# Earlier bank copies, a later second cache batch, and probabilities scaled on VectorE in a hybrid decoder step

## The chip, the cores and the metric

The kernel runs on one core of a Trainium2 chip. The metric is the device time of one execution in microseconds, as the median of several. The engines are named as the profile names them: PE is TensorE, DVE is VectorE, ACT is ScalarE, POOL is GpSimd, and SP is the SyncE queue that issues most transfers.

## What is computed

Two decoder layers over a prompt of 512 tokens and over 8 single sample tokens, each with a paged cache of 256 past tokens. Half of a layer's heads are sparse attention (an indexer picks the keys, 8 heads of 64), half are retention. Cut to what matters:

```
def trunk_layer(x, l, pos, mixer_a, s0, ...):
    h = rmsnorm(x, g_mix_pre[l])
    qa, ka, va, qi, ki, wi, qb, kb, vb, gb = project_mixers(h, w_in[l], pos)   # rope on q and k
    a = mixer_a(qa, ka, va, qi, ki, wi)          # keys by the indexer, then softmax attention
    b, S = retention_mixer(qb, kb, vb, gb, s0, g_ret[l])
    m = jnp.concatenate([a, b], axis=-1) @ w_out[l]
    x = x + rmsnorm(m, g_mix_post[l])
    f = jnp.square(jax.nn.relu(rmsnorm(x, g_ffn_pre[l]) @ w_up[l])) @ w_down[l]
    return x + rmsnorm(f, g_ffn_post[l]), ...

def sparse_attend(q, kg, vg, valid):
    s = einsum('bthd,btkhd->bthk', q, kg) * HEAD_DIM ** -0.5
    p = softmax(where(valid, s, -inf))
    return einsum('bthk,btkhd->bthd', p, vg)
```

The prompt's top 128 scores of each query are found in rounds of eight (a maximum of eight values, then their replacement) and turned into a mask that is added to the attention scores. All numbers are fp32.

## The kernel before

**Chunks and blocks.** The combined input projection is worked off in 8 chunks of 512 columns: 0 indexer, 1 q_a, 2 k_a, 3 v_a, 4 q_b, 5 k_b, 6 gate, 7 v_b. The chunks 0 to 3, 6 and 7 have five blocks, four tiles of 128 prompt tokens and one of the 8 sample tokens, with eight k-steps each (`project`). The chunks 4 and 5 are computed by a Strassen-like scheme with seven products and the sample block, in the order `BLOCKS = (1, 0, 2, 6, 5, 7, 3, 4)` (`project_blocks`); (4,0) is product 1, (4,1) the sample block, (4,2) product 2, and so on. Blocks alternate between two PSUM banks, so block i can start only when block i-2 has been copied out of its bank (`bank_taken`): (4,1) waits for the copy of (3,4), (4,2) for `take_p1(4)`, (5,0) for `chunk_c12(4)` on VectorE, (5,2) for `take_p1(5)`, (5,3) for `evacuate(5, 1)`.

**What runs beside the blocks.** Each engine's order is written out by hand. On TensorE a function `beside_*` is called after every k-step and puts in other work: transposes, the cache batches and the attention of the prompt. The sample tokens' attention goes over two batches of four samples, once for the scores (keys, `beside_v`, L944 and L952) and once for the values (`beside_qb`, L1025). The cache tiles lie in a ring of four (`cring`), so SP loads each next four only when `cache_used` has counted the batch before; key tiles 0 to 3 and 4 to 7, then value tiles 8 to 11, then the weight units 10 and 11, then value tiles 12 to 15, then the state and unit 12 stand in this order on SP's queue.

**Attention steps.** The 32 tiles of prompt attention (4 query blocks of 8 heads) go through 36 steps, spread over `ATT_BLOCKS`, the blocks (4,6) to (6,4). `head_steps(c, i)` gives a block's steps and the k-step behind which each stands: (4,6) has steps 0 and 1 behind k=3 and k=7, (4,7) steps 2 and 3, (5,0) 4 and 5, (5,1) only 6, (5,2) 7 and 8, and so on; (6,0) to (6,3) have four steps each, (6,1) steps 23 to 26, and (6,4) has step 35. The function `attend(i)` on each engine does its share of step i:

- TensorE: for odd i the products with the values of tiles i-5 and i-4 (L970); for even i the scores of tiles i and i+1 (L983); then the transposes of tile i-3 (L993), which wait for `p_ready` and, in the first two, for `om_ready`, the end of `own_values(1)`.
- VectorE: for even i the masks and row maxima of tiles i and i+1 (L1884); then the reciprocal of the row sum of tile i-1 (L1897).
- ScalarE: the copy of the transposed tile i-3 (L1441), the exponential of tile i (L1446), and the scaling of tile i-1 by the reciprocal (L1454), which raises `p_ready`. The last of these, on ScalarE:

```
if 1 <= i <= NT * NH:
    j = i - 1
    p = p_sb[j % P_SLOTS][:, 0:(j // NH + 1) * P]
    act.wait_ge(r_ready, past(r_ready) + j + 1)
    nc.scalar.activation(p, p, ACT.Copy, scale=rinv[:, j % 2:j % 2 + 1]).then_inc(p_ready, 1)
```

A tile is 128 rows by 128, 256, 384 or 512 columns, for query block 0 to 3. Between the steps `beside` puts in other work: on ScalarE the copies of PSUM banks (`take_p1`, `evacuate`, `take_first`, `take_p5`, `scale_quad`), on VectorE the sums of the Strassen scheme (`chunk_*`), the rotations (`rope(c, t)`, four operations), the parts of the gate's sigmoid (`sigmoid(t, part)`: an addition and half of the reciprocal, the other half, the product with the gate) and `decayed_keys`. On GpSimd run the weight sums of the chunks 4 and 5 (L2439) and the gate's products with its gain (L2473).

Every instruction that another one waits for raises a semaphore, and an engine works off its queue in order.

## Time and profile before

| | us |
|---|---|
| median of three runs | 1595.49 (1593.41 to 1599.24) |
| profiled execution | 1598.03 |
| its span | 1596.3 |
| its mean granted TensorE clock | 0.993 |
| PE busy in the span | 1555.8 |
| VectorE, ScalarE, GpSimd busy | 814.3, 488.0, 475.1 |

The profile is one execution, with every instruction's start and duration. Its time is the span and 1.7 us around it. A wait is idle time of an engine, put down to what ended last before the engine went on. TensorE's durations are modelled at their ends, so successive ones overlap a little, and starts are the better measure. The two layers run the same program, the first from the start to about 790 us and the second from there; the stretch of chunks 3 to 6 begins at about 110 us and at about 900 us.

### The profile page before, as it was taken

The page shows a single profiled execution, that of the slowest core. Times are in us where ns is not written, and L with a number is a line of the kernel's source. Part 1 is how long each engine was busy: PE and PEld are TensorE (multiplying, and loading weights), DVE is VectorE, ACT ScalarE, POOL GpSimd, SP SyncE. Part 2 cuts the span into 40 slices and gives each one's busy share as a digit, 9 for nine tenths or more (in the row PEclk, how much of TensorE's full clock was granted, in tenths as well). Part 3 has the DMA queues.
Part 4 walks back from the last instruction along what each step waited for, and adds up shares of the span by engine and source line. Part 5 has one row for each costly group of instructions (what it writes and reads, how often), then busy time and mean ns, then how long its engine had stood idle before and what let it go on. Part 6 is the DMA issues. An engine that isn't in the chain of part 4 may idle for free.

```text
span 1596.3 us, 21682 instructions
## 1 busy us (share of the span) xinstructions
PE 1555.8 (97%) x7966; PEld 1159.2 (73%) x7966; DVE 814.3 (51%) x1644; ACT 488.0 (31%) x1109; POOL 475.1 (30%) x354
## 2 busy tenths in 40 slices
PE   8999899999999999999999998999999999999998
PEld 5445664688888888888844456546888888888887
DVE  4698466864653003333467964578566520133334
ACT  5222366324421002310242224772254210032101
POOL 0005201123564324444310042010236534233461
PEclk9999999999999999999999989999999999999999
DMA  6316310123331222212223263100234321222211
GB/s 222 123 62 214 131 54 1 55 84 106 132 125 61 106 100 85 80 62 97 93 70 106 80 210 108 54 34 22 84 125 139 106 92 68 106 83 102 79 54 54
DMA packets 52812, 150.41 MB, mean 94 GB/s; under 512 B 8250, under 2 KB 29506, under 8 KB 39394
## 3 DMA queue, kind: packets, MB, share of 16 engines
q1 hardware_dynamic: 45218, 140.65, 25.5%
q10 hardware_dynamic: 7488, 8.36, 1.5%
q8 instruction: 64, 1.05, 0.3%
q14 instruction: 42, 0.34, 0.1%
HBM read 139.79 MB, written 9.02 MB: 93 GB/s over the span
## 4 chain that ended last, share of the span: by engine, by line
PE 79%; DVE 13%; ACT 3%; issue 2%; DMA 1%; SPq 1%; POOL 1%; ACTq 0%; DVEq 0%; POOLq 0%
PE ps L1183 45%; PE ps L807 10%; PE ps L1121 7%; PE ps L844 5%; DVE arena L1870 2%; DVE top L1868 2%; PE ps L785 1%; PE ps L772 1%; PE ps L970 1%; PE ps L993 1%; PE ps L983 1%; DVE x_feat L2020 1%; PE ps L1079 1%; ACT arena L1346 1%; DVE arena L1816 1%
## 5 line engine op out<-in xcount | busy, mean ns | idle before, releaser
L807 PE MATMUL ps<-wring,h_feat 128*128 128x512 f32 (+1 forms) x704 | 316.0, 586 | 3.0 <-ACT h_feat L1306 2.2
L1183 PE MATMUL ps<-arena,wring 128*128 128x256 f32 (+1 forms) x1280 | 285.8, 382 | 0.3 <-DVE arena L2104 0.3
L1183 PEld LDWEIGHTS ps<-arena,wring 128*128 128x128 f32 x1280 | 243.0, 190 | 37.8 <-DVE arena L2104 1.1
L807 PEld LDWEIGHTS ps<-wring,h_feat 128*128 128x128 f32 x704 | 124.7, 190 | 125.5 <-issue 112.5
L2403 POOL TENSOR_TENSOR wring<-wring,arena 128x512 f32<-128x512 f32 (+1 forms) x48 | 78.7, 1639 | 346.8 <-PE ps L1183 323.5
L1183 PE MATMUL ps<-h_feat,wring 128*128 128x256 f32 (+1 forms) x768 | 176.6, 381 | 0.0
L1183 PEld LDWEIGHTS ps<-h_feat,wring 128*128 128x128 f32 x768 | 145.9, 190 | 21.6
L1183 PE MATMUL ps<-mix,wring 128*128 128x256 f32 (+1 forms) x512 | 120.3, 383 | 1.5 <-DVE p_sb L2078 1.5
L1183 PE MATMUL ps<-arena 128*128 128x264 f32 x512 | 119.2, 386 | 0.0
L1121 PE MATMUL ps<-mix,wring 128*128 128x256 f32 (+1 forms) x512 | 115.1, 384 | 0.9 <-ACT mix L1473 0.8
L2386 POOL TENSOR_TENSOR pt_sb<-pt_sb 128x256 f32<-128x256 f32 (+1 forms) x94 | 72.7, 773 | 126.5 <-ACT pt_sb L1280 123.0
L1183 PEld LDWEIGHTS ps<-mix,wring 128*128 128x128 f32 x512 | 97.1, 190 | 17.3 <-DVE p_sb L2078 2.3
L1183 PEld LDWEIGHTS ps<-arena 128*128 128x128 f32 x512 | 97.3, 190 | 16.4
L1121 PEld LDWEIGHTS ps<-mix,wring 128*128 128x128 f32 x512 | 96.5, 190 | 15.8 <-issue 1.2
L1346 ACT ACTIVATE arena<-ps,rtok 8x128 f32<-8x128 f32 (+3 forms) x112 | 54.7, 488 | 157.0 <-PE ps L807 148.7
L1514 ACT ACTIVATE arena<-arena 128x264 f32<-128x264 f32 (+1 forms) x96 | 40.6, 423 | 182.9 <-DVE arena L2104 131.7
L2403 POOL TENSOR_TENSOR arena<-wring 128x512 f32<-128x512 f32 (+1 forms) x48 | 79.2, 1650 | 35.0 <-DMA wring<-in_w_all 24.4
L2403 POOL TENSOR_TENSOR wring<-wring 128x512 f32<-128x512 f32 (+1 forms) x48 | 79.6, 1658 | 3.8
L2403 POOL TENSOR_TENSOR arena<-arena,wring 128x512 f32<-128x512 f32 (+1 forms) x48 | 79.2, 1649 | 3.8
L2457 POOL COPY arena<-kTs 128x4 f32<-128x4 f32 x16 | 3.5, 216 | 228.0 <-ACT kTs L1574 219.2
L1491 ACT ACTIVATE p1s<-ps 128x256 f32<-128x256 f32 x40 | 15.4, 385 | 162.2 <-PE ps L1183 162.1
L1183 PE MATMUL ps<-h_feat,arena 128*128 128x264 f32 x256 | 62.2, 386 | 0.0
(251 smaller groups left out, 2106.1 us busy)
## 6 DMA issues: line engine op xcount, KB each, us to landing
wring<-in_w_all SPq DMA_DIRECT2D x108, 1024.0 KB, 5.1
arena<-in_cache_k SPq DMA_DIRECT2D x32, 256.0 KB, 5.2
arena<-in_cache_v SPq DMA_DIRECT2D x32, 256.0 KB, 4.3
o_k_out<-arena ACTq DMA_DIRECT2D x2, 1024.0 KB
o_v_out<-arena ACTq DMA_DIRECT2D x2, 1024.0 KB
arena<-in_state SPq DMA_DIRECT2D x2, 1024.0 KB, 4.8
o_rets_out<-arena ACTq DMA_DIRECT2D x2, 1024.0 KB, 9.6
wring<-in_w_idx SPq DMA_DIRECT2D x3, 648.0 KB, 5.3
```

The source lines that it names most:

```text
L772: last = mm(ps[:, bank_of(0, t), 0:W_IDX], h_feat[:, k, token_cols(t)], wt, start=(k == 0), stop=(k == KD - 1))
L785: last = mm(ps[32 * g:32 * g + NB, bank_of(c, i), 0:c1 - c0], h_feat[:, k, SEQ:TOK], wt[:, (k % 4) * width + c0:(k % 4) * width + c1], sta ...
L807: last = mm(ps[:, bank_of(c, i), 0:width], h_feat[:, k, token_cols(t)], wt, start=(k == 0), stop=(k == KD - 1))
L844: last = mm(product_bank(c, n)[:, t, :], b, a, start=(opens(n) and k == 0), stop=(j == 3), skip_group_check=True)
L1121: last = mm(ps[:, item_bank(n), 0:span(h)], wring[u % SLOTS][:, (m % 2 * KD + k) * P:(m % 2 * KD + k + 1) * P], mix[:, k, HALVES[h]], star ...
L1183: last = mm(out, a[:, j, :], b, start=(opens(n) and j == 0), stop=(j == nk - 1), skip_group_check=True)
L1346: nc.scalar.activation(dst[:, c0:c1], ps[rr, bank_of(c, i), 0:c1 - c0], ACT.Copy, scale=rtok[rr, sc, t:t + 1]).then_inc(done, 1)
L1514: nc.scalar.activation(f, f, ACT.Relu).then_inc(act_step, 1)
L1868: v.max(t8, w).then_inc(dve_step, 1)
L1870: v.match_replace(w, t8, w, MARK).then_inc(dve_step, 1)
L2386: nc.gpsimd.tensor_tensor(ssum[:, hc], ssum[:, hc], sqr[added % 2][:, 0:span(h)], ALU.add).then_inc(sq_used, 1)
L2403: nc.gpsimd.tensor_tensor(dst, in0, in1, op).then_inc(s_ready, 1)
```

## The change

1. TensorE: the second batch of cache scores (`sample_scores(1)`) goes from behind block (3,4) to behind k=3 of (4,0).
2. TensorE: the second batch of cache values goes from behind (4,5) to behind k=5 of (4,6).
3. ScalarE: the copy of block (3,4) goes ahead of the two exponentials of the sample scores. VectorE does nine selection rounds ahead of the maxima of these scores instead of eight, then two, then four instead of five.
4. ScalarE: `take_p1(5)`, `evacuate(5, 1)`, `take_first(5)` and `take_p5(5)` go ahead of the first attention step of their block (`ahead`). In chunk 6 `scale_quad(5, "21")` goes from (6,1) to behind the second step of (6,0). 
5. VectorE: `own_values(1)` goes from ahead of all attention steps to behind step 2, ahead of `chunk_c12(4)`.
6. VectorE: `rope(5, 0)` goes from behind step 23 to behind step 22 and `rope(5, 1)` from behind step 26 to behind step 23; each part of the sigmoid goes one step on.
7. The scaling of the probabilities goes from ScalarE to VectorE, behind the reciprocal; the semaphore `r_ready` falls away.

The diff, without the unchanged body of `sample_scores`:

```
@@ TensorE
-                if (i, k) in ((2, KD - 1), (4, KD - 1)):
-                    g = (i - 2) // 2
+                if (i, k) == (2, KD - 1):
+                    sample_scores(0)
+
+            def sample_scores(g):
...
             def beside_qb(i, k):
+                if (i, k) == (0, 3):
+                    sample_scores(1)
...
-                if (i, k) in ((3, KD - 1), (5, KD - 1)):
-                    g = (i - 3) // 2
+                if (i, k) in ((3, KD - 1), (6, 5)):
+                    g = (i - 3) // 3
@@ ScalarE
-            def beside(c, i):
-
-                if (c, i) == (4, 7):
-                    scale_quad(4, "22", proj_c22)
-                if (c, i) == (5, 0):
-                    scale_quad(4, "12", proj_c12)
+            def ahead(c, i):
+
                 if (c, i) == (5, 1):
                     take_p1(5)
-                    act.wait_ge(as_mm, past(as_mm) + 1)
-                    nc.scalar.activation(mix[:, 0:4, SEQ:TOK], ps[:, 7, 0:4 * NB].rearrange("p (h b) -> p h b", b=NB), ACT.Copy).then_inc(as_read, 1)
-                    act.wait_ge(as_read, up(as_read))
-                    scale_quad(4, "21", proj_c21)
                 if (c, i) == (5, 2):
                     evacuate(5, 1)
                 if (c, i) == (5, 3):
                     take_first(5)
                 if (c, i) == (5, 5):
                     take_p5(5)
-                if (c, i) == (5, 7):
+
+            def beside(c, i, s):
+
+                if (c, i, s) == (4, 7, 0):
+                    scale_quad(4, "22", proj_c22)
+                if (c, i, s) == (5, 0, 0):
+                    scale_quad(4, "12", proj_c12)
+                if (c, i, s) == (5, 1, 0):
+                    act.wait_ge(as_mm, past(as_mm) + 1)
+                    nc.scalar.activation(mix[:, 0:4, SEQ:TOK], ps[:, 7, 0:4 * NB].rearrange("p (h b) -> p h b", b=NB), ACT.Copy).then_inc(as_read, 1)
+                    act.wait_ge(as_read, up(as_read))
+                    scale_quad(4, "21", proj_c21)
+                if (c, i, s) == (5, 7, 0):
                     scale_quad(5, "22", proj_c22)
-                if (c, i) == (6, 0):
+                if (c, i, s) == (6, 0, 0):
                     scale_quad(5, "12", proj_c12)
-                if (c, i) == (6, 1):
-                    evacuate(6, 0)
+                if (c, i, s) == (6, 0, 1):
                     scale_quad(5, "21", proj_c21)
-                if c == 6 and i > 1:
+                if c == 6 and i and s == 0:
                     evacuate(6, i - 1)
...
-                if 1 <= i <= NT * NH:
-                    j = i - 1
-                    p = p_sb[j % P_SLOTS][:, 0:(j // NH + 1) * P]
-                    act.wait_ge(r_ready, past(r_ready) + j + 1)
-                    nc.scalar.activation(p, p, ACT.Copy, scale=rinv[:, j % 2:j % 2 + 1]).then_inc(p_ready, 1)
-                    act.wait_ge(p_ready, up(p_ready))
...
                 evacuate(3, 3)
+                evacuate(3, 4)
                 for g in range(2):
                     act.wait_ge(smx_ready, past(smx_ready) + g + 1)
...
-                evacuate(3, 4)
...
                 for c, i in ATT_BLOCKS:
                     steps = head_steps(c, i)
+                    ahead(c, i)
                     for s, (slot, step) in enumerate(steps):
                         attend(step)
-                        if s == 0:
-                            beside(c, i)
+                        beside(c, i, s)
@@ VectorE
                 if 1 <= i <= NT * NH:
                     j = i - 1
+                    n, c = (j // NH + 1) * P, j % 2
                     dve.wait_ge(p_exp, past(p_exp) + j + 1)
-                    v.reciprocal(rinv[:, j % 2:j % 2 + 1], rsum[:, j % P_SLOTS:j % P_SLOTS + 1]).then_inc(r_ready, 1)
-                    dve.wait_ge(r_ready, up(r_ready))
+                    v.reciprocal(rinv[:, c:c + 1], rsum[:, j % P_SLOTS:j % P_SLOTS + 1]).then_inc(dve_step, 1)
+                    dve.wait_ge(dve_step, up(dve_step))
+                    p = p_sb[j % P_SLOTS][:, 0:n]
+                    v.tensor_scalar(p, p, rinv[:, c:c + 1], None, ALU.mult).then_inc(p_ready, 1)
+                    dve.wait_ge(p_ready, up(p_ready))
...
                 if (c, i, s) == (4, 7, 0):
+                    own_values(1)
                     chunk_c12(4)
...
                     if s == 0:
                         chunk_c21(5)
                         rope(5, NT)
-                    if s in (1, 2):
-                        rope(5, 1 + s)
-                if c == 6 and i and s < 3:
-                    sigmoid(i - 1, s)
+                    else:
+                        rope(5, (None, 2, 3, 0)[s])
                 if (c, i, s) == (6, 1, 0):
-                    rope(5, 0)
-                if (c, i, s) == (6, 1, 3):
                     rope(5, 1)
+                if c == 6 and i and s:
+                    sigmoid(i - 1, s - 1)
...
-                select_top(sc[3], top8[:], 8)
+                select_top(sc[3], top8[:], 9)
...
-                select_top(sc[3], top8[:], 5)
+                select_top(sc[3], top8[:], 4)
...
-                own_values(1)
...
-                        for part in range(len(steps), 3):
+                        for part in range(len(steps) - 1, 3):
                             sigmoid(i - 1, part)
                         decayed_keys(i - 1)
```

## Rows read from the trace of the kernel before

**Rows 1.** First part of the page: busy us, share of the span, instructions
```profile
PE 1555.8 (97%) x7966; PEld 1159.2 (73%) x7966; DVE 814.3 (51%) x1644; ACT 488.0 (31%) x1109; POOL 475.1 (30%) x354
```

**Rows 2.** Waits of PE: line, released by, us in total, times, longest
```profile
PE ps L1025 <- DMA arena<-in_cache_v: 4.5, 2, 2.6
...
PE ps L785 <- ACT arena L1346: 4.1, 2, 2.3
...
PE ps L844 <- ACT arena L1360: 4.0, 2, 2.0
...
PE ps L970 <- ACT pt_sb L1441: 3.9, 6, 1.2
...
PE ps L983 <- DVE neg_mx L1884: 3.0, 2, 1.5
...
PE ps L952 <- DMA arena<-in_cache_k: 1.9, 2, 1.1
```

**Rows 3.** Windows: stretch, us, busy us of each engine, PEclk, DMA share, GB/s
```profile
168.00:171.00 3.00, 2.96 (x16) 0.68 (x16) 0.00 (x0) 0.00 (x0) 0.00 (x0) 0.50 0.00 0
...
936.00:946.00 10.00, 10.00 (x54) 5.62 (x47) 6.71 (x15) 3.22 (x7) 2.34 (x1) 0.50 0.89 338
...
251.50:266.30 14.80, 13.34 (x70) 6.39 (x69) 11.87 (x24) 11.10 (x21) 1.51 (x1) 1.00 0.00 1
```

**Rows 4.** Timeline of PE, layer one: start, duration, operation, count, [idle before, releaser]
```profile
148.83 2.43 PE L844 MATMUL ps<-wring,h_feat 128*128 128x256 f32 x10
...
152.82 3.62 PE L844 MATMUL ps<-arena,mix 128*128 128x256 f32 x16
...
168.04 3.50 PE L1025 MATMUL ps<-arena 128*32 128x512 f32 x16 [2.64 <-DMA arena<-in_cache_v]
...
177.47 0.49 PE L983 MATMUL ps<-arena 64*128 64x128 f32 x4
...
179.83 1.92 PE L844 MATMUL ps<-wring,h_feat 128*128 128x256 f32 x8
...
191.03 3.12 PE L844 MATMUL ps<-wring,h_feat 128*128 128x256 f32 x8 [2.01 <-ACT arena L1360]
...
198.15 1.99 PE L844 MATMUL ps<-arena,mix 128*128 128x256 f32 x8 [0.29 <-ACT arena L1346]
...
203.52 1.99 PE L844 MATMUL ps<-arena 128*128 128x256 f32 x8
```

**Rows 5.** Timeline of PE, layer two
```profile
947.92 3.62 PE L844 MATMUL ps<-arena,mix 128*128 128x256 f32 x16
...
962.38 1.92 PE L1025 MATMUL ps<-arena 128*32 128x512 f32 x16 [1.89 <-DMA arena<-in_cache_v]
```

**Rows 6.** Timeline of ACT, layer one, then layer two
```profile
143.25 1.54 ACT L1346 ACTIVATE arena<-ps,rtok 8x128 f32<-8x128 f32 x4
...
146.29 0.60 ACT L1360 ACTIVATE arena<-ps 128x512 f32<-128x512 f32 x1 [1.49 <-issue]
...
935.98 0.60 ACT L1360 ACTIVATE arena<-ps 128x512 f32<-128x512 f32 x1 [1.00 <-ACT arena L1346]
```

**Rows 7.** Timeline of DVE, layer one
```profile
127.92 0.69 DVE L1868 MAX8 top<-arena 128x8 f32<-128x512 f32 x1
...
140.06 0.42 DVE L2237 TENSOR_REDUCE mxs<-ps 128x1 f32<-128x257 f32 x1
...
178.95 0.69 DVE L1841 TENSOR_TENSOR arena<-ps,arena 128x512 f32<-128x512 f32 x1
...
190.21 0.93 DVE L1810 TENSOR_TENSOR rstd_ffn<-arena,sinT 128x256 f32<-128x256 f32 x1
```

**Rows 8.** Groups: count | busy us, mean ns | idle before, releaser
```profile
L1454 ACT ACTIVATE p_more<-p_more,rinv 128x512 f32<-128x512 f32 x8 | 5.8, 724 | 6.4 <-DVE rinv L1897 6.2
...
L1856 DVE TENSOR_SCALAR arena<-s_sb,wi 128x512 f32<-128x512 f32 x2 | 1.0, 486 | 0.7 <-ACT s_sb L1548 0.7
```

**Rows 9.** Timeline of POOL, layer one
```profile
188.52 2.34 POOL L2439 TENSOR_TENSOR wring<-wring 128x1024 f32<-128x1024 f32 x1 [21.62 <-PE ps L785]
```

More of the change, by code:

```diff
@@ L240 @@
     stat_mm=6, st_mm=168, tok_std=6, proj_read=32, proj_p1=2, proj_c11=2, proj_p5=2, proj_u2=2, proj_u3=2, proj_c22=2, proj_c12=2,
-    proj_c21=2, proj_scaled=6, in_sums=4, chunk_sums=8, r_ready=32, tr_read=19, ts_read=3, dot_read=12, srelu_done=1,
+    proj_c21=2, proj_scaled=6, in_sums=4, chunk_sums=8, tr_read=19, ts_read=3, dot_read=12, srelu_done=1,
     wm_ready=1, sp_exp=2, vrep_ready=2, spt_ready=1, p_exp=32, pt_ready=32, as_read=1, blk_read=4, gate_exp=5,
@@ L446, in build @@
         chunk_sums = sem("chunk_sums")
-        r_ready = sem("r_ready")
         rope_done = sem("rope_done")
@@ L938, in beside_v @@
                     transpose_group(zr[0], *pairs[2 + k // 2])
-                if (i, k) in ((2, KD - 1), (4, KD - 1)):
-                    g = (i - 2) // 2
-                    if g == 0:
-                        pe.wait_ge(sbias_ready, past(sbias_ready) + 1)
-                    mm(ps[:, 2 + g, 0:L], exps[:, g, :], bias_s[:], start=True, stop=False, skip_group_check=True)
-                    for b in range(4 * g, 4 * g + 4):
-                        pe.wait_ge(c_slot[b % CSLOTS], past(c_slot[b % CSLOTS]) + 16 * NPAGES * (b // CSLOTS + 1))
-                        pe.wait_ge(knew_done, past(knew_done) + b + 1)
-                    for h in range(4):
-                        for b in range(4 * g, 4 * g + 4):
-                            q4 = 32 * (b % 4)
-                            kc = cring[b % CSLOTS][:].rearrange("p (h k) -> p h k", k=L)
-                            last = mm(ps[q4:q4 + 32, 2 + g, 0:L], qs[:, b, 32 * h:32 * h + 32], kc[:, h, :],
-                                      start=False, stop=(h == 3), skip_group_check=True)
-                            if h == 3:
-                                last.then_inc(cache_used, 1)
+                if (i, k) == (2, KD - 1):
+                    sample_scores(0)
+            def sample_scores(g):
+                if g == 0:
+                    pe.wait_ge(sbias_ready, past(sbias_ready) + 1)
+                mm(ps[:, 2 + g, 0:L], exps[:, g, :], bias_s[:], start=True, stop=False, skip_group_check=True)
+                for b in range(4 * g, 4 * g + 4):
+                    pe.wait_ge(c_slot[b % CSLOTS], past(c_slot[b % CSLOTS]) + 16 * NPAGES * (b // CSLOTS + 1))
+                    pe.wait_ge(knew_done, past(knew_done) + b + 1)
+                for h in range(4):
+                    for b in range(4 * g, 4 * g + 4):
+                        q4 = 32 * (b % 4)
+                        kc = cring[b % CSLOTS][:].rearrange("p (h k) -> p h k", k=L)
+                        last = mm(ps[q4:q4 + 32, 2 + g, 0:L], qs[:, b, 32 * h:32 * h + 32], kc[:, h, :],
+                                  start=False, stop=(h == 3), skip_group_check=True)
+                        if h == 3:
+                            last.then_inc(cache_used, 1)
             def attend(i):
```

## The prediction

> **What bounds the kernel now.** I read the busy times first: TensorE (PE) is busy 97% of the span, VectorE 51%, ScalarE 31% [rows 1]. So time can only come out of TensorE's idle stretches and out of stretches where its clock is low. The waits of PE come next [rows 2]. In the part that the change touches (chunks 3 to 6 of the projection, about 135 to 285 us in the first layer and 925 to 1078 us in the second) six of them sum to 4.5 + 4.1 + 4.0 + 3.9 + 3.0 + 1.9 = 21.4 us over both layers; total less longest gives the other layer's share. Then the windows: behind the wait at 166 us the granted clock was 0.50 (the 1.2 GHz level) for 3 us, and in the second layer it was 0.50 over all of 936 to 946 us [rows 3]. The timeline gives the price of that: 16 products of L1025 took 3.50 us behind the 2.64 us wait at 168.04, and 1.92 us at full clock in the second layer [rows 4, 5]. The waits before the low stretches were 2.0 (twice), 2.3 and 2.6 us; the 1.8 us wait of the first layer at 144.9 and the 1.9 us one at 962.4 had none behind them. A wait of 2 us or more thus costs more than itself here.
>
> **The change part by part.** (c,i) is block i of chunk c. Terms are per layer.
>
> *A, opening of chunk 4.* The second batch of cache scores moves behind four of eight k-steps of (4,0), about 1.9 us later, which hides its wait for the key cache (1.1 and 0.8 us) [rows 2]. The copy of (3,4) moves ahead of the two exponentials; before, TensorE waited for it at (4,1) (1.8 and 2.3 us) [rows 2]. That would bring (4,2) forward to 148.83 - 1.1 - 1.8 = 145.9 [rows 4]. What is late next is take_p1(4), which frees the bank of (4,2). ScalarE reached it at 146.29 [rows 6]. The exponentials now come one selection round later, (140.06 - 127.92)/8 = 1.52 us [rows 7]; the four pieces of the copy, 1.54 us, leave the queue between them and take_p1 [rows 6]. The two cancel: take_p1(4) still starts at 146.3, ends at 146.85, and (4,2) starts at 146.9, with a new wait of 1.0 us. Gain 1.9 us in layer one. In layer two take_p1(4) started at 935.98 [rows 6], so (4,2) can start at 936.6 and (4,3) after the undisturbed length 152.82 - 148.83 = 4.0 us, at 940.6 instead of 947.92 [rows 4, 5]: gain 7.3 us, most of it the low clock. The value cache's transfers wait for the batch and leave 0.7 us later; the first group that needs them stands some 14 us behind, which covers that. The weight units 10 and 11 queued behind them on SP's queue are needed later still.
>
> *B, second value batch,* from behind (4,5) to k=5 of (4,6). Four k-steps (1.99 us), the step-0 products (0.49) and two k-steps more (1.0) stand in between, 3.4 us, against a wait of 2.6 and 1.9 us [rows 2, 4]. Its transfers are started by the first value batch, which moves with TensorE, so the wait goes and some 0.8 us is to spare. Gain: 2.64 + (3.50 - 1.92) = 4.2 us in layer one, 1.9 us in layer two [rows 4, 5].
>
> *C, own_values(1)* moves from ahead of the attention steps to behind step 2 on VectorE, ahead of chunk_c12(4). Behind it wait the first transposes on TensorE (step 3) and, behind those, (5,0), whose bank chunk_c12(4) frees. Before, step 2 started at 177.47, chunk_c12(4) on VectorE at 178.95, (5,0) at 179.83 [rows 4, 7]. Now 0.33 us of scaling (two more rows down) and 1.44 us of own_values (two operations of 0.69 with gaps) stand ahead of chunk_c12(4) and its 0.69: it ends 1.48 + 0.33 + 1.44 + 0.69 = 3.95 us after step 2, and (5,0) starts at 4.0 instead of 2.36. Loss 1.7 us, as 1.0 us ahead of the transposes and 0.6 behind them.
>
> *D, banks copied ahead.* take_p1(5), evacuate(5,1), take_first(5) and take_p5(5) no longer stand behind the copy and exponential of their first step. Before, take_p1(5) started only after step 6, and (5,2) waited 2.0 us in both layers [rows 2, 4]. Now its product is done one block (about 4 us) before (5,2), and it ends some 2 us early. The price is that the attention copies stand behind them: evacuate(5,1), 1.54 us [rows 6], delays the copy of step 7. TensorE needs that copy two steps later (5 us), so it is covered. Behind the wait (5,2) ran low: 8 products in 3.12 us against 1.99, and block (5,2) lasted 198.15 - 191.03 = 7.12 us against 203.52 - 198.15 = 5.37 for (5,3), which does the same [rows 4]. Gain 2.01 + 1.75 = 3.8 us, and the second layer repeats it.
>
> *E, chunk 6: scaling on VectorE, rotations ahead of the sigmoid.* ScalarE loses 32 scalings per layer, 0.73 us at 512 columns [rows 8]. The nearest row for them on VectorE is the multiply by a column at L1856, 0.49 us for 512 [rows 8]; I put 0.29, 0.35, 0.42 and 0.49 for the four widths, 12.4 us per layer, where VectorE idles about half the time. Upper bound: 0.69, what a two-input operation of that size takes [rows 7]. The waits here were 3.0 us for VectorE's maxima and 3.9 us for ScalarE's copies, over both layers [rows 2]. The first stood behind a sigmoid part and a rotation between steps 23 and 24; now only a rotation (about 2.2 us) stands there and step 24's maxima precede the sigmoid. The second arose because ScalarE's scaling waited for VectorE's reciprocal (6.2 us of such waits at L1454 [rows 8]) with the next copy behind it; that link is gone. Load: block (6,2) took 14.8 us with TensorE busy 13.34, VectorE 11.87 and ScalarE 11.10 [rows 3]. Afterwards ScalarE has 11.1 - 4 x 0.73 = 8.2 and VectorE 11.87 + 4 x 0.49 less the rotation and one decayed-keys product that fell in there (2.9) = 10.9, both under 13.3. Gain 3.4 us per layer. Behind chunk 6 everything shifts along.
>
> VectorE and GpSimd disturb each other here: a 256-column operation took 0.93 us at 190.21, beside a GpSimd operation of 2.34 us from 188.52, where one of 512 columns took 0.69 [rows 7, 9]. The Trainium skill (SBUF — State Buffer, Who interferes with whom) says why this speaks against the change: a tensor_scalar in a two-port mode takes a port pair shared with GpSimd, and the later of the two blocks until the other ends. By that rule, which the 0.93 us row bears out, a scaling may stand up to 2.3 us behind each gate multiply; one per block would fill VectorE to 13.2 of 13.3 us, the case of rival 2.
>
> **Sum.** A 1.9 + 7.3, B 4.2 + 1.9, C -1.7 twice, D 3.8 twice, E 3.4 twice: 9.2 + 6.1 - 3.4 + 7.6 + 6.8 = 26.3 us. Against the profiled execution's own time, 1598.0 us (span 1596.3), that is 1571.7. This execution was 2.5 us above the median 1595.5; if it was so for the low clock that goes away, 1571.7 stands, otherwise it is 1569.2. I take 1570.5.
>
> **Rivals.**
> 1. *The low clock comes back.* The new waits (1.0 us at (4,2); 1.0 and 0.6 us around step 3, both beside narrow products) may count together as the 2 us waits did. For: 2.3 us cost about 5 us of clock in layer two. Against: single waits of 1.8 and 1.9 us cost none. Price 1.6 us at two places in two layers, or 5 us once or twice: about 1577. Chance 0.15.
> 2. *VectorE becomes the bound of chunk 6.* Scaled probabilities stand behind 2.3 us of sigmoid or rotation in its queue; the transposes need them two steps later (6 us), which speaks against. Then E is lost: 1570.5 + 6.8 = 1577. Chance 0.15.
> 3. *The early copies aren't early,* since ScalarE arrives late at them: D is lost and the time is 1578. Chance 0.06.
> 4. *Slower than before.* Handing each probability tile over through VectorE's in-order queue delays every step. With 64 steps, the gain of 26 is used up at 0.41 us per step, and at 0.54 the kernel is over 0.5% slower; at 0.6 us, 1570.5 + 38 = 1609. Against it: the two steps of slack, and that VectorE is busy for half of the time [rows 1]. Chance 0.04.
> 5. Several of 1 to 3 with a wait that I don't see: 1590, no change. Chance 0.06.
>
> **Numbers.** My forecast has 0.54. The range 1564 to 1581 takes in rivals 1 to 3 and, below, C costing nothing (3.4 us) and the lower of the two baselines. A measurement of this kernel can tell about 0.5% from no change. Faster by more than that: 0.54 + 0.15 + 0.15 + 0.06 = 0.90; same 0.06; slower 0.04.
>
> **What would show it.** A: PE's waits for L1346 at (4,1) and for the key cache are gone, a wait of about 1 us for L1360 stands at (4,2), and no 10 us stretch at 0.50 follows. B: no wait at L1025, between two parts of (4,6). C: about 1 us of wait for VectorE at the first transposes and 0.6 us at (5,0). D: no wait at (5,2), whose first 8 products take 2.0 us. E: no waits in chunk 6, scalings of 0.49 us at 512 columns, ScalarE's busy time down by 36 us and VectorE's up by 25. It is wrong if waits for the scaled tiles stand ahead of L993, or if the low clock moves to another place.

## The result and the profile after

The changed kernel took 1572.1 us (median of four runs, 1570.8 to 1573.1) where the kernel before, on the same chip, took 1594.5. The ratio is 0.9863, interval 0.983 to 0.990. On another chip it was 1572.0 against 1592.6, ratio 0.987 (0.984 to 0.991). That is 20.6 to 22.4 us less. The forecast was 1570.5. One execution of one experiment's kernel took 9200 us and is left out of its median; the executions of each kernel otherwise lie within 1% of each other.

The kernel before varies more than the changed one: 23 executions of it on one chip took 1586.0 us (mean granted clock 1.000) to 1601.0 us (0.989). Part of what the two traces below differ by is therefore low clock that many other executions of the kernel before do not have.

The profiled execution took 1573.14 us, 24.9 less than that of before; its span is 1571.4 and its mean granted clock 0.999. First the page's busy times, then the waits of PE in the stretch that was changed, in the columns of [rows 1] and [rows 2].

```profile
PE 1547.7 (98%) x7966; PEld 1154.9 (73%) x7966; DVE 845.1 (54%) x1708; ACT 450.0 (29%) x1045; POOL 476.1 (30%) x354
...
PE ps L994 <- DVE arena L2151: 2.0, 2, 1.0
PE ps L971 <- ACT pt_sb L1447: 1.7, 2, 0.9
PE ps L843 <- ACT arena L1363: 1.4, 2, 1.2
...
PE ps L843 <- DVE arena L1841: 0.8, 2, 0.4
...
PE ps L843 <- DVE arena L1823: 0.4, 2, 0.2
```

The six waits of [rows 2] summed to 21.4 us; these five stand here now, with 6.3. The engines did what was meant: ScalarE lost 38.0 us (36 forecast), VectorE gained 30.8 (25 forecast). (Lines have moved: the copies of L1360 are at L1363, the products of L844 at L843, L1025 is L1028.)

The timeline of PE in the changed kernel, in the columns of [rows 4], first of layer one and then of layer two:

```profile
146.28 2.42 PE L843 MATMUL ps<-wring,h_feat 128*128 128x256 f32 x10 [0.22 <-ACT arena L1363]
...
150.64 3.62 PE L843 MATMUL ps<-arena,mix 128*128 128x256 f32 x16
...
166.36 1.92 PE L1028 MATMUL ps<-arena 128*32 128x512 f32 x16
...
169.18 1.89 PE L843 MATMUL ps<-wring,arena 128*128 128x256 f32 x8
...
174.43 0.30 PE L994 MATMUL ps<-idn,p_sb 128*128 128x128 f32 x1 [1.01 <-DVE arena L2151]
175.15 1.96 PE L843 MATMUL ps<-wring,h_feat 128*128 128x256 f32 x8 [0.42 <-DVE arena L1841]
...
184.22 1.89 PE L843 MATMUL ps<-wring,h_feat 128*128 128x256 f32 x8
...
189.20 1.89 PE L843 MATMUL ps<-arena,mix 128*128 128x256 f32 x8
...
250.23 1.09 PE L971 MATMUL ps<-pt_sb,arena 128*64 128x128 f32 x16 [0.85 <-ACT pt_sb L1447]
...
269.63 0.66 PE L856 MATMUL ps<-idn,arena 128*128 128x128 f32 x4
...
924.69 3.85 PE L843 MATMUL ps<-wring,h_feat 128*128 128x256 f32 x10 [1.17 <-ACT arena L1363]
```

Differences of starts give what each term of the prediction became. The marks are the first instruction behind (3,4), the starts of (4,3), (4,7), (5,0) and (5,3), and the first transposes of chunk 7. B begins at the end of (4,5) before and at the start of (4,6) after; that start stands 0.16 us ahead of the modelled end of (4,5), so B's gains may be 0.16 us too small.

| stretch | layer one: before, after, gain | layer two: before, after, gain | forecast gains |
|---|---|---|---|
| A: behind (3,4) to (4,3) | 17.03, 14.88, 2.2 | 22.23, 17.22, 5.0 | 1.9, 7.3 |
| B: behind (4,5) to (4,7) | 10.25, 6.12, 4.1 | 7.92, 6.12, 1.8 | 4.2, 1.9 |
| C: (4,7) to (5,0) | 4.18, 5.97, -1.8 | 4.19, 5.98, -1.8 | -1.7, -1.7 |
| D: (5,0) to (5,3) | 18.32, 14.05, 4.3 | 18.37, 14.05, 4.3 | 3.8, 3.8 |
| E: (5,3) to the transposes of chunk 7 | 83.23, 80.43, 2.8 | 83.19, 80.45, 2.7 | 3.4, 3.4 |

The gains sum to 23.6 us against 26.3 forecast; 1.3 us more lie elsewhere (0.3 of them by the marks of B). Of these 0.7 are a wait of the feed-forward part (L1183 before, L1186 after, released by L2078 and L2082), which fell from two times 0.75 us to one. That is not the change's doing: a second trace of the changed kernel has it twice again (1.5 us), and the experiments' kernels have it never, once or twice.

### The profile page after: what moved, and what is told of

The parts are those of the page before. It is cut to its first block, busy times and chain, and to the rows that moved or that the text cites. A ratio compares the mean times of both kernels' runs of the same rounds, so it can differ in the third digit from the quotient of the medians.

```text
span 1571.4 us, 21618 instructions
## 1 busy us (share of the span) xinstructions
PE 1547.7 (98%) x7966; PEld 1154.9 (73%) x7966; DVE 845.1 (54%) x1708; ACT 450.0 (29%) x1045; POOL 476.1 (30%) x354
## 4 chain that ended last, share of the span: by engine, by line
PE 77%; DVE 18%; issue 2%; ACT 2%; POOL 0%; DMA 0%; ACTq 0%; DVEq 0%; POOLq 0%
PE ps L1186 46%; PE ps L806 9%; PE ps L1124 7%; PE ps L843 4%; DVE arena L1870 3%; DVE top L1868 3%; PE ps L771 1%; DVE x_feat L2024 1%; PE ps L784 1%; DVE arena L1814 1%; DVE arena L1816 1%; PE ps L971 1%; DVE rstd_ffn L1812 1%; PE ps L1082 1%; PE ps L994 1%
## 5 line engine op out<-in xcount | busy, mean ns | idle before, releaser
L1186 PE MATMUL ps<-arena,wring 128*128 128x256 f32 (+1 forms) x1280 | 285.8, 382 | 0.3 <-DVE arena L2108 0.3
L1186 PEld LDWEIGHTS ps<-arena,wring 128*128 128x128 f32 x1280 | 243.0, 190 | 37.7 <-DVE arena L2108 1.1
L1186 PE MATMUL ps<-h_feat,wring 128*128 128x256 f32 (+1 forms) x768 | 176.6, 381 | 0.0
L1186 PEld LDWEIGHTS ps<-h_feat,wring 128*128 128x128 f32 x768 | 145.9, 190 | 21.6
L1186 PE MATMUL ps<-mix,wring 128*128 128x256 f32 (+1 forms) x512 | 120.2, 383 | 0.8 <-DVE p_sb L2082 0.8
L1186 PE MATMUL ps<-arena 128*128 128x264 f32 x512 | 119.1, 386 | 0.0
L1186 PEld LDWEIGHTS ps<-arena 128*128 128x128 f32 x512 | 97.3, 190 | 16.4
L1186 PEld LDWEIGHTS ps<-mix,wring 128*128 128x128 f32 x512 | 97.2, 190 | 16.3 <-DVE p_sb L2082 1.2
L2405 POOL TENSOR_TENSOR arena<-wring 128x512 f32<-128x512 f32 (+1 forms) x48 | 79.4, 1653 | 35.2 <-DMA wring<-in_w_all 24.9
L2405 POOL TENSOR_TENSOR wring<-wring 128x512 f32<-128x512 f32 (+1 forms) x48 | 79.5, 1656 | 3.8
L1186 PE MATMUL ps<-h_feat,arena 128*128 128x264 f32 x256 | 62.2, 386 | 0.0
L1186 PE MATMUL ps<-mix,arena 128*128 128x264 f32 x256 | 62.2, 386 | 0.0
```

The costliest lines, as they stand in the source:

```text
L1186: last = mm(out, a[:, j, :], b, start=(opens(n) and j == 0), stop=(j == nk - 1), skip_group_check=True)
L2405: nc.gpsimd.tensor_tensor(dst, in0, in1, op).then_inc(s_ready, 1)
```

## The experiments

Each starts from the changed kernel or from the one before and changes one thing, except where the text says otherwise. The times of the changed kernel that they are set against are 1572.1 and 1572.0. None undoes part A, the new opening of chunk 4: what A gained is read from the two traces alone.

### One edit of chunk 6 undone at a time

Scaling back on ScalarE:

```diff
+                if 1 <= i <= NT * NH:
+                    act.wait_ge(r_ready, past(r_ready) + j + 1)
+                    nc.scalar.activation(p, p, ACT.Copy, scale=rinv[:, j % 2:j % 2 + 1]).then_inc(p_ready, 1)
...
-                    v.tensor_scalar(p, p, rinv[:, c:c + 1], None, ALU.mult).then_inc(p_ready, 1)
```

> The changed kernel with the scaling of the probabilities back on ScalarE, behind VectorE's reciprocal; all else as changed. My theory (TensorE's waits in chunk 6 had two causes, VectorE's late maxima and ScalarE's copies behind its scaling): only the second returns, 0.5 to 2 us per layer over the changed kernel's 1572.1, so 1573 to 1576, with waits for ScalarE's copies at L971 and no waits for the maxima. Rival one (the scaling on VectorE is the whole of chunk 6's 2.8 us per layer): 1577.7, and both kinds of waits. Rival two (GpSimd blocking the scalings costs more than they bring): below 1571.

1569.87 us (1568.5 to 1570.8): 2.2 less than with the scaling on VectorE, the opposite of what the prediction's step E says. The number is that of my second rival; its mechanism was hardly seen (four scalings, below). Between (5,3) and the transposes of chunk 7 it takes 79.5 us, 0.95 less than the changed kernel; one wait is left there:

```profile
261.21 1.09 PE L972 MATMUL ps<-pt_sb,arena 128*64 128x128 f32 x16 [0.48 <-ACT pt_sb L1448]
...
268.42 0.66 PE L857 MATMUL ps<-idn,arena 128*128 128x128 f32 x4
```

The sigmoid's quarters ahead of the rotations again:

```diff
-                    else:
-                        rope(5, (None, 2, 3, 0)[s])
-                if (c, i, s) == (6, 1, 0):
-                    rope(5, 1)
-                if c == 6 and i and s:
-                    sigmoid(i - 1, s - 1)
+                    if s in (1, 2):
+                        rope(5, 1 + s)
+                if c == 6 and i and s < 3:
+                    sigmoid(i - 1, s)
+                if (c, i, s) == (6, 1, 0):
+                    rope(5, 0)
+                if (c, i, s) == (6, 1, 3):
+                    rope(5, 1)
```

> The changed kernel with the rotations and the sigmoid's parts in the old order on VectorE. My theory: the 1.5 us wait of the score products for the maxima returns in each layer, at steps 24 to 26, and the copies' wait stays near its 0.85: 1575. Rival (with the scaling gone from ScalarE, the maxima are no longer what is late): 1572, no wait for the maxima. Rival two (VectorE, now with the scalings, is the bound of chunk 6 in the old order): over 2.5 us per layer, above 1577.

1575.27 us (1572.6 to 1576.4): 3.2 more. Two waits for VectorE's maxima are back, 2.1 us together, where I had expected one of 1.5; the copies' wait fell to 0.16 instead of staying at 0.85. The timeline of PE of this kernel:

```profile
241.58 1.13 PE L984 MATMUL ps<-arena 64*128 64x512 f32 x4 [0.93 <-DVE neg_mx L1884]
...
255.88 1.13 PE L984 MATMUL ps<-arena 64*128 64x512 f32 x4 [1.16 <-DVE neg_mx L1884]
```

### The square, and the same two edits on the kernel before

Both edits undone, the rest of the change kept:

> The changed kernel with both edits of chunk 6 undone: the scaling on ScalarE and the sigmoid's quarters ahead of the rotations again; the other edits stay. It closes a square: both edits 1572.0 us, scaling undone 1569.9, order undone 1575.3. Theory 1 (the order gains 3.2 us, the scaling on VectorE costs 2.1, each by itself): 1573.1 us (1572.4 to 1574). Theory 2, the step of the prediction (the two are needed together, since ScalarE and VectorE are late in turn in chunk 6): 5.6 us more than with both, by the two traces between block (5,3) and the first transposes of chunk 7, so 1577 us or more.

1574.8 us (1573.8 to 1576.3, five executions). With the scaling on ScalarE the new order is worth 4.9 us (1574.8 to 1569.9), with it on VectorE 3.3. Neither theory had that: it lies between 1573.1 and 1577. PE's waits in chunk 6 of layer one are those of the kernel before, and go together to a single 0.48 us once the order is changed:

```profile
240.08 1.13 PE L985 MATMUL ps<-arena 64*128 64x512 f32 x4 [1.57 <-DVE neg_mx L1891]
243.63 0.88 PE L972 MATMUL ps<-pt_sb,arena 128*64 128x128 f32 x12 [0.23 <-ACT pt_sb L1448]
251.41 1.09 PE L972 MATMUL ps<-pt_sb,arena 128*64 128x128 f32 x16 [1.22 <-ACT pt_sb L1448]
264.13 1.09 PE L972 MATMUL ps<-pt_sb,arena 128*64 128x128 f32 x16 [0.47 <-ACT pt_sb L1448]
```

So the 1.2 us that PE waited for ScalarE's copy went though ScalarE still scales. Moving the scaling instead also takes them (1.92 us of such waits here, 0.16 in the experiment before), but then the waits for the maxima grow from 1.57 to 2.09 us. Either edit removes the copies' waits; only the order removes both kinds.

The kernel before with the scaling on VectorE and nothing else:

> The kernel before, with nothing but the scaling of the probabilities moved to VectorE. It takes 1592.6 to 1594.5 us. Theory 1 (VectorE is the later engine in chunk 6, and the scaling beside GpSimd's operation takes 1.2 to 2.1 us in place of 0.3 to 0.4): 1 to 4 us slower, 1594 to 1598. Theory 2, from the prediction: the waits for ScalarE's copies of transposed probabilities, 1.9 us per layer, and part of the 2.0 us before block (5,3) go, and VectorE has room: 4 us faster, 1589 to 1590.

1585.5 us against 1591.0 beside it, ratio 0.997 (0.995 to 0.999). There the scaling gains 5.4 us, and my second thoughts after the first experiment (Theory 1) were wrong. By the traces 1.74 us per layer lie behind (5,3), where the copies' waits fall from 1.95 to 0.16 us and those for the maxima grow from 1.48 to 2.10; 0.44 us is the wait at (5,2), and the rest, 1.9 us in layer one and 0.4 in layer two, is a lower loss of clock behind it. That wait in the timeline of PE of this kernel:

```profile
194.38 1.99 PE L843 MATMUL ps<-wring,h_feat 128*128 128x256 f32 x8 [1.57 <-ACT arena L1359]
```

and in that of ScalarE in the kernel before, where a scaling stands right ahead of the copy that frees the bank:

```profile
189.95 0.40 ACT L1454 ACTIVATE p_sb<-p_sb,rinv 128x128 f32<-128x128 f32 x1
190.38 0.60 ACT L1360 ACTIVATE arena<-ps 128x512 f32<-128x512 f32 x1
```

Without it the wait is 2.01 - 0.43 = 1.6 us. With the copy ahead of the step, as in the change, there is no wait and no low clock at (5,2), and this part of the gain cannot be made.

The kernel before with both edits:

> The kernel before with the scaling on VectorE and the rotations ahead of the sigmoid's quarters, without the banks copied ahead, without the earlier batches and without the new opening of chunk 4. The prediction gives the two 3.4 us per layer, 6.8 together: 1586 to 1588 us. By the square of the changed kernel (3.2 gained, 2.1 lost): 1591.5 to 1593.4. If it gains more than that, the scaling is worth something where ScalarE is the later engine, as it is ahead of the copies of chunk 5's banks, and part of the gain there can be had by either edit.

1589.2 us, ratio 0.999 (0.997 to 1.001): with both the gain is not to be told from nothing, and the median is 3.7 above that with the scaling alone. The new order moves `rope(5, 0)` ahead of step 23, but here `scale_quad(5, "21")`, which it reads, still stands in (6,1) on ScalarE; the change moved it to (6,0) in its part 4. The rotation waits 4.21 us for it, and two rotations run together, with a scaling behind the first and the maxima of the next step behind the second. Timeline of VectorE in this kernel:

```profile
240.97 0.54 DVE L1803 TENSOR_TENSOR rstd_ffn<-arena,sinT 128x256 f32<-128x256 f32 x1 [4.21 <-ACT arena L1374]
...
243.65 0.42 DVE L1894 TENSOR_SCALAR p_more<-p_more,rinv 128x384 f32<-128x384 f32 x1
...
246.48 0.69 DVE L1877 CUSTOM_DVE_ANT_0 s_sb<-ps,arena 128x512 f32<-128x512 f32 x1
```

ScalarE scales that quad from 239.82 to 240.87 us. It is the quad and not the copies of the banks that is missing: the next experiment has the banks copied late and the quad early, and takes 79.98 us from (5,3) to chunk 7, against 83.42 here.

Eight kernels in one measure, from the start of (5,0) to the first transposes of chunk 7. "Part 4" is the banks copied ahead together with the quad "21" in (6,0); the kernels without it also lack the other parts of the change, which lie ahead of (5,0):

| part 4 | scaling | order | layer one | layer two | median us |
|---|---|---|---|---|---|
| no (before) | ScalarE | old | 101.55 | 101.56 | 1594.5, 1593.5, 1592.6, 1591.0 |
| no | VectorE | old | 97.43 | 99.01 | 1585.5 |
| no | VectorE | new | 99.36 | 99.36 | 1589.2 |
| quad only | VectorE | new | 97.46 | 97.44 | 1577.5 |
| yes | ScalarE | old | 96.75 | 96.75 | 1574.8 |
| yes | VectorE | old | 95.89 | 95.90 | 1575.3 |
| yes | ScalarE | new | 93.53 | 93.52 | 1569.9 |
| yes (changed) | VectorE | new | 94.48 | 94.50 | 1572.0 |

Per layer the scaling on VectorE is worth +4.1 or +2.6 us alone, about 2.2 of which is not clock (1.74 and 0.44), +0.9 with part 4, and -1.0 with part 4 and the new order.

### The copies of chunk 5's banks behind the first step again

```diff
-                    ahead(c, i)
                     for s, step in enumerate(steps):
...
+                        if s == 0:
+                            ahead(c, i)
                         beside(c, i, s)
```

> The changed kernel, with the copies of chunk 5's banks on ScalarE behind the attention step of their block again (steps 4, 5, 6, 8). My theory: per layer the wait before block (5,3) of 2.0 us and the low clock behind it come back, 4.3 us by the difference of the two traces between (5,0) and (5,3), so 1572.1 + 8.6 = 1580.7 us (1579 to 1582). A rival: only the clock's loss is at stake and the sigmoid's new place already has ScalarE ahead there, so that the wait returns at 1 us or less and without the low clock: 1574 to 1575. A third: the copies ahead of the steps also set later steps back, so undoing it gives part of it back: 1576 to 1578.

1577.5 us (1573.4 to 1579.4), 5.5 more, between my theory and its first rival and inside the range of the third. From (5,0) to chunk 7 both layers take 97.4 us, 3.0 more than the changed kernel. From (5,0) to (5,3) it is 17.47 us, 3.4 more than the changed kernel's 14.05; 0.4 of that comes back behind (5,3), the third rival's mechanism in small. The wait at (5,2) is back at 1.57 us, the 0.44 us of the scaling short of 2.01, and the clock behind it was low in both layers. The timeline of PE in layer one:

```profile
186.17 2.90 PE L843 MATMUL ps<-wring,h_feat 128*128 128x256 f32 x8 [1.57 <-ACT arena L1363]
```

and the window behind it, in the columns of [rows 3]:

```profile
188.00:190.00 2.00, 2.00 (x9) 1.01 (x8) 1.38 (x2) 0.00 (x0) 0.00 (x0) 0.50 0.00 0
```

### The value batch and the own values at their old places

```diff
-                if (i, k) in ((3, KD - 1), (6, 5)):
-                    g = (i - 3) // 3
+                if (i, k) in ((3, KD - 1), (5, KD - 1)):
+                    g = (i - 3) // 2
...
-                    own_values(1)
                     chunk_c12(4)
...
                 chunk_c22(4)
+                own_values(1)
```

> The changed kernel, with the second batch of the value cache and the second group of own values at their old places. My theory: the own values ahead of the last transposes cost 1.8 us per layer (a gain here), the batch one block earlier costs a wait for the cache pages that the second layer of the kernel before showed too: 1.7 us there and 2.6 us in the first layer, plus 1.5 us of low clock in the first layer. As TensorE is now ahead by the 2.2 and 5.0 us that the opening of chunk 4 gave, the wait is longer by that, unless the transfers start earlier too: bounds of the batch 4.1 + 1.8 = 5.9 us and 5.9 + 7.2 = 13.1 us; minus 3.6. So 1574.4 to 1581.6, middle 1577. A rival: the pages come as much earlier as TensorE does and only the wait as such returns, with the gain of the own values as large: 1572 to 1573, no difference.

1574.8 us (1571.6 to 1578.2), the low end of my theory; the four executions also cover the rival's range, and the profiled one is only 0.9 us above that of the changed kernel. The waits in the two layers' timelines:

```profile
165.64 2.48 PE L1028 MATMUL ps<-arena 128*32 128x512 f32 x16 [2.16 <-DMA arena<-in_cache_v]
...
945.10 1.92 PE L1028 MATMUL ps<-arena 128*32 128x512 f32 x16 [1.87 <-DMA arena<-in_cache_v]
```

They are no longer than in [rows 4, 5], since the transfers start earlier with TensorE: in layer one SP issued this group from 156.38 us on, and from 158.31 in the kernel before. The first has the low clock behind it (2.48 against 1.92 us for the batch). The own values at their old place cost nothing: no wait at L994 or at (5,0).

### The two waits that the change itself made

Own values one step earlier, between the steps of (4,6):

```diff
+                if (c, i, s) == (4, 6, 1):
+                    own_values(1)
                 if (c, i, s) == (4, 7, 0):
-                    own_values(1)
                     chunk_c12(4)
```

> The changed kernel with the second own_values one step earlier, behind step 1, where VectorE idled 4.6 us. My theory: the wait at the first transposes (1.0 us) and the one at block (5,0) (0.4 us) go, with the shift behind them 1.8 us per layer: 1568.5. Rival (own_values waits for the value batch and then holds up the maxima of step 2): 1572 or more, with the wait now at the scores or the transposes.

1570.67 us (1569.3 to 1571.5), 1.4 less. Both waits are gone, but in this execution low clock stood behind a wait of 0.2 us at (4,2) and took 1.7 us back: ten products in 4.11 us, 2.42 in the changed kernel.

```profile
145.59 4.11 PE L843 MATMUL ps<-wring,h_feat 128*128 128x256 f32 x10 [0.21 <-ACT arena L1363]
```

The transfers of the value outputs behind the first copies of chunk 4, with one selection round moved between the places where VectorE does them:

```diff
-                act.dma_start(v_out[...]...)
-                act.dma_start(vs_out[...]...)
                 take_p1(4)
                 act.wait_ge(vrep_mm, past(vrep_mm) + 1)
...
+                act.dma_start(v_out[...]...)
+                act.dma_start(vs_out[...]...)
```

> The changed kernel with eight selection rounds ahead of the sample maxima (and five later) and with the two transfers of v issued behind the first bank copies of chunk 4 instead of ahead of them. My theory: the wait at (4,2) (0.2 and 1.2 us) goes and with it the low clock behind it in the second layer (block (4,2) lasted 5.7 us there against 4.0), 3 us in all: 1569. Rival (the low clock comes from the narrow products around it, not from the wait): block (4,2) of layer two still runs low and only 1.4 us are gained: 1570.7. Rival two (what is late at (4,2) is something else on ScalarE or VectorE): no change, 1572.

1570.29 us (1569.2 to 1570.6), 1.8 less. The wait at (4,2) and the low clock are gone in both layers. Which of the two edits did it was not tested: ScalarE starts `take_p1(4)` here at 142.82 and 920.65 us, so far ahead of (4,2), at 145.58 and 923.42, that by these times even the longest issues seen here (0.41 and 1.56 us) would just have fitted in front of it. Of the 1.07 us that layer one had gained by (4,3), 0.75 was lost in the feed-forward part, where two element-wise operations of VectorE took 2.51 and 2.00 us; the same two took 0.43 and 1.15 us in the changed kernel. In the second trace of the changed kernel they took 2.58 and 2.00 us, so this is not the experiment's doing either. Timeline of VectorE in this experiment:

```profile
470.25 2.51 DVE L2063 TENSOR_TENSOR arena<-arena 128x264 f32<-128x264 f32 x1
...
473.26 2.00 DVE L2066 TENSOR_TENSOR arena<-arena 128x256 f32<-128x256 f32 x1
```

GpSimd's:

```profile
470.11 2.36 POOL L2405 TENSOR_TENSOR arena<-arena,wring 128x1024 f32<-128x1024 f32 x1
```

and PE's:

```profile
475.78 3.77 PE L1186 MATMUL ps<-mix,wring 128*128 128x264 f32 x16 [0.75 <-DVE p_sb L2082]
```

The first of the two, started 0.1 us after GpSimd's operation, ends at 472.76 and GpSimd's at 472.47.

### The changed kernel again

> The changed kernel itself, beside the other runs, as the point from which they are measured. It took 1572.1 us (1570.8 to 1573.1). Theory 1 (the difference of 2.2 us between it and the kernel that scales on ScalarE is real): 1571 to 1573.5 here. Theory 2 (that difference was one between chips): 1569.9, where the other one lay. Its trace should again show the wait at block (4,2) of the second layer at about 0.2 us or about 1.2 us; with the long one the granted clock goes to 0.50 behind it.

1572.0 us (1571.6 to 1572.6), so the 2 us are not the chip's. Its low clock at (4,2) stood in the first layer this time, behind a wait of 0.20 us, and not in the second behind one of 0.58. I had expected it behind the long wait of the second layer.

### A version put together

Scaling on ScalarE, own values one step earlier, the transfers behind the copies with the selection round moved, and `block_out` (a finished attention block's copies on ScalarE) behind the copy of transposed probabilities:

```diff
-                if i >= 12 and (i - 12) % NH == 0:
-                    block_out((i - 12) // NH)
...
                     act.wait_ge(pt_ready, up(pt_ready))
+                if i >= 12 and (i - 12) % NH == 0:
+                    block_out((i - 12) // NH)
```

> A version put together from the experiments so far: the changed kernel with the scaling back on ScalarE (1569.9 us), the own values between the steps of block (4,6), the transfers of the value outputs behind the first copies of chunk 4, and ScalarE's writing of a finished attention block behind the copy that TensorE waits for. Waits that should go, summed over the two layers, by the trace of the first of these: L995 1.4, L844 for VectorE 0.9, L844 for ScalarE 0.5, and of the 1.0 at L972 all or part. My theory: 1569.9 - 3.3 = 1566.6 us (1566 to 1567.5). The rival: as with the two edits alone, half of it returns, at the start of block (4,2) as low clock or in the feed-forward part, where VectorE's element-wise work beside GpSimd's comes late by another 0.8 us: 1568 to 1569.

1563.3 us (1562.0 to 1564.8), ratio to before 0.982 (0.978 to 0.985), the fastest here and 8.7 below the changed kernel. It beat my figure by 3.3: from (4,7) to (5,0) it takes 4.18 us (167.62 to 171.80), 1.47 less than the version with the scaling on ScalarE alone, where I had counted the two waits, 1.1; and (4,2) starts at 145.09, 1.3 us earlier in layer one, where I had counted 0.3. Of the waits in this part only this one is left per layer, and the clock is at 1.00 throughout chunk 4:

```profile
258.07 1.09 PE L972 MATMUL ps<-pt_sb,arena 128*64 128x128 f32 x16 [0.47 <-ACT pt_sb L1446]
```

The same version with the scaling on VectorE:

> The combined version that took 1563.3 us, with the scaling on VectorE as in the changed kernel, and nothing else different. Theory 1 (the scaling on VectorE costs 2.1 us, most of it in chunk 6 and at the first transposes of block (4,2)): 1565.4 us (1564.8 to 1566.5). Theory 2 (its price was that of the waits before the last transposes and before (5,0), which this version no longer has): 1563 us, no difference.

1565.0 us (1563.9 to 1566.0), 1.7 more, on another chip than its pair, and 1.9 more by the two spans (1564.2 and 1562.3). But 1.0 us of that stands ahead of (4,2) of layer one (146.10 against 145.09), where no tile has been scaled yet. From (4,7) to the first transposes of chunk 7 the scaling costs 0.68 and 0.66 us, where it costs 1.27 and 1.31 between the changed kernel and the one with the scaling on ScalarE. So the truth lies between the two theories: part of the price was that of waits that this version no longer has.

## Why the prediction was right, and where it was not

The forecast of 1570.5 us was 1.6 below the 1572.1 measured, and most parts came as worked out.

**B, C and D** did. B: no wait at L1028, which now takes 1.92 us in both layers. C: 1.01 and 0.42 us of waits where 1.0 and 0.6 were named, 1.8 us lost against 1.7. D: a gain of 4.3 us against 3.8. I took 5.37 us, the length of (5,3), for an undisturbed (5,2), and it takes 4.98 (184.22 to 189.20); that is 0.4 of the difference. Undoing D alone cost 3.4 us in this stretch; of the missing 0.9 the scaling is 0.44 of the wait, and block (5,2) took 6.66 us there against 7.12 [rows 4].

**A** was right in layer one (2.2 for 1.9) and too large in layer two (5.0 for 7.3). The step that failed is the clock: I took a wait of about 1.0 us at (4,2) to leave it alone, from waits of 1.8 and 1.9 us that had none behind them. In this execution low clock stood behind the 1.17 us wait and cost 1.7 us in block (4,2) beside the wait itself (the row at 924.69 above; ten products in 3.85 us); the other 0.6 us is `take_p1(4)`, which came later than I had it. The prediction's rule, that a wait of 2 us or more costs more than itself and a shorter one does not, fails both ways: in the second trace of the changed kernel the low clock stands behind 0.20 us and not behind 0.58, and in the kernel before with the scaling on VectorE a wait of 2.12 us at (4,1) of layer two had none behind it. The 7.3 us, "most of it the low clock", was thus in good part the price of one execution of the kernel before. The window behind the wait of 1.17 us:

```profile
926.00:928.00 2.00, 2.00 (x6) 1.55 (x6) 1.90 (x5) 1.36 (x4) 0.05 (x1) 0.50 1.01 414
```

This is rival 1 at one of its four places (at the others the clock stayed). Why the wait was 1.17 in one layer and 0.22 in the other stands in ScalarE's timeline: the issue of the second value output took 0.43 us in layer one and 1.42 in layer two, and take_p1(4) stands behind it. In the kernel before it had taken 1.00 and 0.50 us; the prediction left the issue out and kept take_p1(4) where it was, at 146.3, while it started at 145.63. (In the experiment with the own values earlier it was 1.56 us in layer two, with a wait of 1.35.)

```profile
145.16 0.43 ACTq L1587 DMA_DIRECT2D o_vs_out<-arena  x1
...
922.57 1.42 ACTq L1587 DMA_DIRECT2D o_vs_out<-arena  x1
924.04 0.60 ACT L1363 ACTIVATE arena<-ps 128x512 f32<-128x512 f32 x1 [1.94 <-PE ps L784]
```

**E** had nearly the right size (2.8 for 3.4) for a reason that was half wrong. I laid the 3.9 us of waits for ScalarE's copies on its scaling and wanted the scaling on VectorE for it; the square shows that the new order takes them and the maxima's waits alone, 96.75 to 93.53 us, and that the scaling then costs 1.0. With the order old the scaling did gain, 0.9 us. It costs, as far as the traces tell, because VectorE becomes the late one: over 190 to 270 us it is busy 67.8 us with it and 57.4 without, at 9.2 to 9.5 of 10 us in five of the eight windows of ten, and the sum of chunk 5 at L1823 ends 2.05 us later with it (199.68 against 197.63), which is the new wait of 0.20 us at (5,5). That is rival 2 in part, 0.95 us per layer where it had put 3.4. I had compared the loads of one block, 10.9 against 13.3 us, and an average does not show the queue.

What the prediction said of VectorE and GpSimd bore on this, though the 0.93 us row that it leaned on was of a two-input operation and not of a scaling. A scaling beside a GpSimd operation took 1.20 us where others of its size took 0.29, and one of the sliding-window probabilities 2.12 us where the one ahead of it took 0.36. Timeline of VectorE in the changed kernel:

```profile
146.08 0.36 DVE L2249 TENSOR_SCALAR p1s<-p1s,ris 128x257 f32<-128x257 f32 x1
...
146.67 2.12 DVE L2249 TENSOR_SCALAR p1s<-p1s,ris 128x257 f32<-128x257 f32 x1
...
185.12 1.20 DVE L1901 TENSOR_SCALAR p_sb<-p_sb,rinv 128x128 f32<-128x128 f32 x1
```

and of GpSimd:

```profile
146.25 2.40 POOL L2441 TENSOR_TENSOR wring<-wring 128x1024 f32<-128x1024 f32 x1 [3.35 <-PE ps L784]
...
183.88 2.36 POOL L2441 TENSOR_TENSOR wring<-wring 128x1024 f32<-128x1024 f32 x1 [19.15 <-PE ps L784]
```

Each long one ends with GpSimd's: 148.79 against 148.65, 186.32 against 186.24. By the Trainium skill (SBUF — State Buffer, Who interferes with whom), the later of the two blocks until the other ends; this trace agrees to 0.15 us. But only four of the 64 scalings were caught, at 1.13 to 1.20 us, all outside chunk 6, so it was not what decided; the prediction had one per block. The 2.12 us operation did cost something that I had not looked for: TensorE's transposes behind it started at 148.85, and block (4,2) took 4.36 us in layer one against 4.0 in the layers where neither this nor the clock held it up.

**The other rivals.** The early copies were early (rival 3 out), and TensorE's products waited for no handed-over tile but those behind the own values; only its weight loads, which run ahead of the products, waited 7.5 us in 18 places for scaled tiles (rival 4 out: the worst effect of the scaling is 1.0 us per layer, not 0.6 us per step). That the forecast is only 1.6 us off owes something to luck: the sum was 2.7 us too high, for A in layer two and E, and 1.3 us outside the stretch, at least half of it chance, made up for half of it.

## What to carry to other kernels

When two engines are late in turn, try each of several edits against the others, not only against the kernel before: the scaling was worth about 2 us a layer alone, beside what the clock made of it, and cost 1 once the copies stood ahead and the order was right. When an operation is moved earlier, move what it reads as well: the rotation ahead of its quad cost what the new order should have gained. Ask of a wait for an engine whether that engine had itself been waiting, since a better order may then do without moving its load. Put a copy that frees a bank ahead of what can stand behind it in its queue. Compare stretches of traces, not only medians: a single wait that comes and goes (0.75 us) or a fall of the clock (1.4 us and more) is as large as the effect of a small edit.

## What the runs showed of the hardware that I had not expected

- The granted clock did not follow the length of the wait. At (4,2) it fell to 0.50 behind waits of 0.20, 0.21, 0.26, 1.17 and 1.35 us and stayed at 1.00 behind 0.20, 0.22, 0.24, 0.29, 0.38, 0.40, 0.58 and 0.67 us, in executions of kernels that are the same up to there but for small shifts; ahead of all of these stand the narrow products of the cache scores and of the tokens. Before (5,2) a wait of 1.57 us had it twice in one kernel, once in another and in neither layer of a third. In the three kernels that have no wait in the opening of chunk 4 at all it never fell there. In the kernels with the old opening, which wait at (4,1) instead, it fell behind 2.10, 2.27 and 2.31 us and not behind 1.52, 1.77 and 2.12. At (4,2), behind a wait there, a fall cost 1.4 to 1.7 us in the ten products behind it (3.85 and 4.11 us against 2.42). What decides was not settled.
- The issue of the same transfer on ScalarE's queue took 0.42 to 1.56 us.
- Beside a GpSimd operation of 2.4 us, a VectorE operation of 0.3 to 0.4 us took up to 2.6 us, in a stretch that no edit touched. TensorE's wait of 0.75 us behind such a place came none, one or two times per execution, also between two executions of the same kernel.
